# The chunked recurrence of a hybrid encoder block: one group for all transposes of a chunk, and a new order of the groups in a turn

## The chip, the cores and the metric

The kernel runs on one core of a Trainium2 chip. The metric is the device time of one execution in microseconds (us), here the median of three runs. The profile is one further execution with the hardware profiler on.

## The reference, cut to what matters

One layer for 2048 tokens of width 1024: a combined projection, then attention on one half of the columns and a recurrence (RWKV7) on the other, an output projection, and a mixture of experts. The change lies in the recurrence alone. For each of 8 heads (64 values, 64 keys) the reference steps through the tokens:

```
def step(state, inp):
    r_t, w_t, k_t, v_t, kk_t, b_t = inp
    sa = jnp.einsum('bhvk,bhk->bhv', state, -kk_t)
    state = (state * w_t[:, :, None, :] + sa[..., None] * b_t[:, :, None, :]
             + v_t[..., None] * k_t[:, :, None, :])
    return state, jnp.einsum('bhvk,bhk->bhv', state, r_t)
```

## The kernel before

The stages run one after the other: projection, attention, recurrence (`recur`), merge with the router, experts. Everything is float32.

`recur` cuts the 2048 tokens into 32 chunks of 64 (C = 64). Inside a chunk the recurrence is written as 64x64 matrix products: products of the chunk's own data, a triangular system that is solved by blocks and squarings (groups r1 to r8), and a few products with the running state. The eight heads are held as four pairs. Each product of one head works on 64 of TensorE's rows, and its result goes to 64 of its columns, so that several heads run at once in different quarters of the array. Products that contract over all 128 partitions use two column halves, and products with 128 result rows use two row halves. So there are three tile shapes: 64x64 (up to four at once), 64x128 (two at once) and 128x64 (two at once).

The work is laid out as a software pipeline. In turn k (k from -3 to 31) four chunks are in work: S_ = k (state step), B_ = k+1 and A_ = k+2 (two parts of the solve), N_ = k+3 (first products). A turn is full when all four exist, which holds for k = 0 to 28. The order of the groups in a turn is written by hand in `PE_TURN`, `ACT_TURN` and `DVE_TURN`. The code follows these orders, and each group of matmuls raises one semaphore at its last matmul. `counts` turns the orders into the semaphore values that the others wait for.

The groups, as the code of `turn` on TensorE has them:

| name | chunk | products | tile shape | reads, and who takes the result |
|---|---|---|---|---|
| s0 | B_ (before) | 8 | 64x64 | masked key term times values, opens the accumulation |
| s1 | S_ | 8 | 64x64 | adds state times A; ScalarE copies to sa0 |
| s2 | S_ | 8 | 64x64 | solve (q5) times sa0; ScalarE and VectorE copy to sv |
| s3 | S_ | 8 | 128x64 | tbk times sv; VectorE adds the old state (ds), then st scales it |
| y1, y2 | S_ | 8, 8 | 64x64, 128x64 | output term of the state, then of sv; ScalarE copies y |
| gl, gbk | N_ | 8, 8 | 64x64, 64x128 | first products; VectorE masks both (gl, g) |
| bk | A_ | 8 | 64x128 | transposes of B and K of a head together; ScalarE copies to tbk |
| v | A_ | 4 | 128x64 | transposes of V; ScalarE copies to sv |
| r1, r2, r3q, r3l, r4 | A_ | 16, 16, 8, 8, 8 | 64x64 | first part of the solve; copies and adds on ScalarE and VectorE |
| r5, r6, r7, r8 | B_ | 16, 8, 16, 8 | 64x64 | second part; r5 and r7 copied by ScalarE to ty, r6 and r8 added by VectorE |

Four PSUM tensors (ba, bb, bc, bd) of two banks each rotate by one place at each turn: what was bd is ba in the next turn, ba becomes bb, and bb becomes bc. r8 and r3l both write the low part of ba. gl of the next turn writes the same tensor under the name bb, and s0 of the next turn writes what r4 wrote as bd. This gives the waits:

```
if live(k):
    pe.wait_ge(s_dve, on_dve["r8", k])      # ahead of gl
...
if live(A_):
    pe.wait_ge(s_dve, on_dve["r4", A_])     # ahead of s0
```

GpSimd adds the identity to a part of g (`w0`) once a turn. SyncE loads a chunk's inputs into one of 5 buffers (`cin`) as soon as y1 and st of the chunk five earlier are done. Every product goes through the helper `product`, so all matmuls of the recurrence stand under line 937 in the profile; copies of ScalarE stand under L1112, additions of VectorE under L1147.

Of the kernel before, what the change touches and what calls it, by code (L numbers as in the profile page):

```python
# [24 lines left out]
P = 128  # L25
# [600 lines left out]
def attend(nc, io, dr, keep):  # L626
    with ExitStack() as ctx:
# [143 lines left out]
        def _(dve):  # L771
# [51 lines left out]
PE_TURN = (("s1", 0), ("gl", 3), ("r5", 1), ("gbk", 3), ("bk", 2), ("r1", 2), ("s2", 0), ("r2", 2), ("s3", 0), ("v", 2), ("r6", 1),  # L823
           ("r3q", 2), ("r3l", 2), ("r7", 1), ("y1", 0), ("r4", 2), ("y2", 0), ("r8", 1), ("s0", 1))
ACT_TURN = (("s1", 0), ("r5", 1), ("bk", 2), ("r1", 2), ("sa", 0), ("r2", 2), ("v", 2), ("r3l", 2), ("r7", 1), ("y", 0))
DVE_TURN = (("gl", 3), ("gbk", 3), ("sa", 0), ("r2", 2), ("s3", 0), ("r6", 1), ("st", 0), ("r3q", 2), ("r4", 2), ("r8", 1))
# [11 lines left out]
def recur(nc, io, dr, keep, ahead):  # L838
    with ExitStack() as ctx:
# [9 lines left out]
        tbk = [m.sb(f"tbk{n}", [P, 2, NPAIR, C]) for n in range(RINGS["tbk"])]  # L849
# [39 lines left out]
        def keys(couple):  # L889

            return couple.rearrange("p (r a) n -> p r (a n)", r=2)[:, :, 0:NPAIR * C]

        def values(couple, rows):

            return couple[rows, 1::2, 0:2 * C]

# [35 lines left out]
        def _(pe):  # L932
            A, R, V = slice(0, C), slice(C, 2 * C), slice(4 * C, 5 * C)
# [23 lines left out]

            def turn(k):
# [3 lines left out]
                ga, gn, gs = (g[c % RINGS["g"]] for c in (A_, N_, S_))  # L962
                if live(S_):
                    if S_ > 0:
                        pe.wait_ge(s_dve, on_dve["st", S_ - 1])
                    pe.wait_ge(s_pe, on_pe["s0", S_])
                    for p, r, f, t, u, j in by_features():
                        ins = product(ba[t, j, LO], xs[f, p, A], state[S_ % 2][f, p, :], False, not first(p))
                    ins.then_inc(s_pe, 1)
                if live(N_):  # L970
                    pe.wait_ge(s_ld[N_ % LOADS], 16 * (N_ // LOADS) + 16)
                    if live(k):
                        pe.wait_ge(s_dve, on_dve["r8", k])
                    for p, r, f, t, u, j in by_features():
                        ins = product(bb[t, j, LO], xn[f, p, A], xn[f, p, b_of(p)])
                    ins.then_inc(s_pe, 1)
                if live(B_):
                    pe.wait_ge(s_dve, on_dve["r4", B_])
                    if live(k - 1):
                        pe.wait_ge(s_act, on_act["y", k - 1])  # L980
                    elif live(k + 1):
                        pe.wait_ge(s_act, on_act["v", k + 1])
                    l = gl[B_ % RINGS["gl"]]
                    for p, r, f, t, u, j in by_features():
                        product(bc[f, p, LO], q2[t, j, :], eye[t, :])
                        ins = product(bc[f, p, HI], l[t, j, 1, :], q2[t, j, :])
                    ins.then_inc(s_pe, 1)
                if live(N_):
                    for p, r, f, t, u, j in by_features():
                        ins = product(whole(bd)[:, r, p, :], xn[f, p, BK], xn[f, p, AR])  # L990
                    ins.then_inc(s_pe, 1)
                if live(A_):
# [4 lines left out]
                    for p, r, f, t, u, j in by_features():  # L997
                        ins = product(keys(bb)[:, r, p * C:(p + 1) * C], xa[f, p, BK], eye[f, :])
# [20 lines left out]
                if live(A_):  # L1019
                    pe.wait_ge(s_act, on_act["r1", A_])  # L1020
                    pe.wait_ge(s_w0, A_ + 1)
                    if live(N_):
                        pe.wait_ge(s_dve, on_dve["gbk", N_])
                    w = w2[A_ % 2]
                    for q in range(2):
                        for r in range(2):
                            for h in range(2):
                                p, r, f, t, u, j = head(q + 2 * h, r)
                                product(bd[t, j, 0:2 * C], w[t, j, 0:C], w[t, j, C:3 * C])
                            for h in range(2):  # L1030
                                p, r, f, t, u, j = head(q + 2 * h, r)
                                ins = product(bd[t, j, 2 * C:3 * C], w[t, j, C:2 * C], w[t, j, 0:C])
                    ins.then_inc(s_pe, 1)
                if live(S_):
                    pe.wait_ge(s_act, on_act["sa", S_])
                    pe.wait_ge(s_dve, on_dve["sa", S_])
                    for p, r, f, t, u, j in by_features():
                        ins = product(ba[f, p, LO], tbk[S_ % RINGS["tbk"]][:, r, p, :], sv[S_ % RINGS["sv"]][:, p, features(r)])
                    ins.then_inc(s_pe, 1)
                if live(A_):  # L1040
                    for p in (0, 2, 1, 3):
                        u = HALVES[1 - p // 2]
                        ins = product(values(bb, u)[:, p % 2, :], xa[:, p, V], ident[:, :])
                    ins.then_inc(s_pe, 1)
                if live(B_):
                    pe.wait_ge(s_act, on_act["r5", B_])
                    if live(A_):
                        pe.wait_ge(s_act, on_act["r1", A_])
                    for p, r, f, t, u, j in by_features():
                        ins = product(bc[t, j, LO], ty[0][f, p, LO], ty[0][f, p, HI])  # L1050
# [12 lines left out]
                if live(B_):  # L1063
                    pe.wait_ge(s_dve, on_dve["r6", B_])
                    l = gl[B_ % RINGS["gl"]]
                    for p, r, f, t, u, j in by_features():
                        product(bc[f, p, LO], q3[t, j, :], eye[t, :])
                        ins = product(bc[f, p, HI], l[t, j, 2, :], q3[t, j, :])
                    ins.then_inc(s_pe, 1)
                if live(S_):  # L1070
                    if live(A_):
                        pe.wait_ge(s_act, on_act["v", A_])
                    for p, r, f, t, u, j in by_features():
                        ins = product(bb[f, p, LO], state[S_ % 2][f, p, :], xs[f, p, R], first(p), False)
                    ins.then_inc(s_pe, 1)
                if live(A_):
# [4 lines left out]
                    ins.then_inc(s_pe, 1)  # L1081
                if live(S_):
                    pe.wait_ge(s_pe, on_pe["y1", S_])
                    for p, r, f, t, u, j in by_features():
                        ins = product(bb[f, p, LO], sv[S_ % RINGS["sv"]][:, p, features(r)], gs[:, r, p, HI], False, not first(p))
                    ins.then_inc(s_pe, 1)
                if live(B_):
                    pe.wait_ge(s_act, on_act["r7", B_])
                    if not live(A_) and live(S_):
                        pe.wait_ge(s_dve, on_dve["s3", S_])  # L1090
                    for p, r, f, t, u, j in by_features():
                        ins = product(ba[t, j, LO], ty[1][f, p, LO], ty[1][f, p, HI])
                    ins.then_inc(s_pe, 1)
                    pe.wait_ge(s_act, on_act["v", B_])
                    if live(A_):
                        pe.wait_ge(s_dve, on_dve["r4", A_])
                    for p, r, f, t, u, j in by_tokens():
                        ins = product(bd[t, j, LO], g[B_ % RINGS["g"]][u, r, p, LO], sv[B_ % RINGS["sv"]][u, p, features(r)],
                                      first(p), False)
# [8 lines left out]
        def _(act):  # L1108
# [6 lines left out]
            def turn(k):  # L1115
                S_, B_, A_ = k, k + 1, k + 2
                ba, bb, bc, bd = banks(k)
                top, low = HALVES
                if live(S_):
                    copy("s1", S_, (sa0[:, :, :], ba[:, :, LO]))  # L1120
                if live(B_):
                    copy("r5", B_, (ty[0][:, :, :], bc[:, :, PAIR]))
                if live(A_):
                    copy("bk", A_, (tbk[A_ % RINGS["tbk"]].rearrange("p r a n -> p r (a n)"), keys(bb)))
# [4 lines left out]
                if live(A_):  # L1129
                    act.wait_ge(s_dve, on_dve["r2", A_])  # L1130
                    copy("r2", A_, (w4[:, :, :, :], bd.rearrange("p a (x y n) -> p a x y n", x=2, y=2)[:, :, :, 0, :]))
                    v = sv[A_ % RINGS["sv"]]
                    copy("v", A_, (v[low, 0:2, :], values(bb, low)), (v[top, 2:4, :], values(bb, top)))
                    copy("r3l", A_, (l8[:, :, :], ba[:, :, LO]))
                if live(B_):
                    copy("r7", B_, (ty[1][:, :, :], bc[:, :, PAIR]))
                if live(S_):
# [6 lines left out]
        def _(dve):  # L1144
# [4 lines left out]
            def turn(k):  # L1149
# [20 lines left out]
                if live(S_):  # L1170
                    add("s3", S_, ds_, ba[:, :, LO], state[S_ % 2])
                if live(B_):
                    add("r6", B_, q3, bc[:, :, LO], q2)
                if live(S_):
                    dve.wait_ge(s_dve, on_dve["s3", S_])
# [3 lines left out]
                if live(A_):  # L1179
                    dve.wait_ge(s_dve, on_dve["r2", A_])  # L1180
                    add("r3q", A_, q1, bd[:, :, LO], q0)
                    dve.wait_ge(s_dve, on_dve["r3q", A_])
                    add("r4", A_, q2, bd[:, :, LO], q1)
                if live(B_):
                    dve.wait_ge(s_dve, on_dve["r6", B_])
                    add("r8", B_, q5[B_ % 2], ba[:, :, LO], q3)

# [988 lines left out]
```

## Time and profile before

| | |
|---|---|
| median of three runs | 2983.03 us (2982.71 to 2984.04) |
| the profiled execution's own time | 2979.28 us |
| its span in the profile | 2977.3 us |
| mean granted TensorE clock | 0.981 of full speed |
| recurrence in the span | from about 1277 to 1680 us |
| state updates (st), first and last start | 1312.7 and 1679.5 us |
| a full turn | 12.04 us where nothing disturbs it |

The profiled execution agrees with the median within 0.13%. In the profile a matmul of float32 shows as two records, so a group of 8 products is x16. The line of a group names output, then moving operand, then stationary operand. PE is the matmul row of TensorE and PEld its weight loads. Ends of matmuls are modelled; starts are records.

### The profile page before, as it was taken

The page shows a single profiled execution, that of the slowest core. Times are in us where ns is not written, and L with a number is a line of the kernel's source. Part 1 is how long each engine was busy: PE and PEld are TensorE (multiplying, and loading weights), DVE is VectorE, ACT ScalarE, POOL GpSimd, SP SyncE. Part 2 cuts the span into 40 slices and gives each one's busy share as a digit, 9 for nine tenths or more (in the row PEclk, how much of TensorE's full clock was granted, in tenths as well). Part 3 has the DMA queues.
Part 4 walks back from the last instruction along what each step waited for, and adds up shares of the span by engine and source line. Part 5 has one row for each costly group of instructions (what it writes and reads, how often), then busy time and mean ns, then how long its engine had stood idle before and what let it go on. Part 6 is the DMA issues. An engine that isn't in the chain of part 4 may idle for free. (4 is left out here: it accounts for less than half of the span.)

```text
span 2977.3 us, 61430 instructions
## 1 busy us (share of the span) xinstructions
PE 2824.1 (95%) x23130; PEld 1777.5 (60%) x23131; DVE 1541.1 (52%) x3560; ACT 979.8 (33%) x2303; POOL 644.8 (22%) x812
## 2 busy tenths in 40 slices
PE   8999999999979999989999799994999999999999
PEld 6787878778756666679998555452333333333333
DVE  4677676777768988834444577763111111111111
ACT  3343344334437777734444333331000000000000
POOL 0000000000015555611111001002333333333333
PEclk9999999999989999999999999996999999999999
DMA  7111121121130110041111132253889788787663
GB/s 253 61 64 60 48 79 56 50 72 60 52 116 1 44 44 1 1 169 60 62 57 57 45 113 91 94 183 94 286 301 339 249 299 314 276 292 246 251 218 124
DMA packets 187586, 393.03 MB, mean 132 GB/s; under 512 B 15866, under 2 KB 74106, under 8 KB 186576
## 3 DMA queue, kind: packets, MB, share of 16 engines
q1 hardware_dynamic: 166848, 339.34, 33.0%
q0 software_dynamic: 20512, 50.54, 4.9%
q8 instruction: 159, 2.61, 0.4%
q14 instruction: 67, 0.55, 0.1%
HBM read 325.22 MB, written 78.22 MB: 136 GB/s over the span
## 5 line engine op out<-in xcount | busy, mean ns | idle before, releaser
L328 PE MATMUL pj_big<-pj_xnT,pj_w_in 128*128 128x256 f32 x2816 | 634.6, 381 | 2.1 <-DVE pj_xnT L467 1.5
L328 PEld LDWEIGHTS pj_big<-pj_xnT,pj_w_in 128*128 128x128 f32 x2816 | 537.0, 191 | 83.2 <-issue 5.7
L1921 PE MATMUL ex_pgu<-keep_res,ex_xT 128*64 128x512 f32 x2560 | 568.5, 597 | 0.0
L1921 PEld LDWEIGHTS ex_pgu<-keep_res,ex_xT 128*64 128x64 f32 x2560 | 177.1, 137 | 334.5 <-issue 334.5
L2029 DVE TENSOR_TENSOR ex_hh<-ex_sg,ex_pgu 128x256 f32<-128x256 f32 x80 | 33.7, 421 | 583.5 <-ACT ex_sg L1994 583.5
L1939 PE MATMUL ex_py<-keep_res,ex_hT 128*64 128x512 f32 x1280 | 288.3, 592 | 1.0 <-DVE ex_yb L2037 1.0
L767 POOL TENSOR_SCALAR at_tt<-at_e,at_cf 128x512 f32<-128x512 f32 (+3 forms) x160 | 219.7, 1376 | 176.7 <-DVE at_pd L811 164.1
L1440 PE MATMUL mg_po<-keep_res,mg_mix 128*128 128x512 f32 x512 | 232.5, 611 | 6.9 <-DVE mg_mix L1743 6.9
L298 POOL TENSOR_TENSOR pj_m<-pj_qn,pj_cosin 128x256 f32<-128x256 f32 x64 | 46.6, 729 | 823.4 <-DVE pj_qn L528 597.0
L1994 ACT ACTIVATE ex_sg<-ex_pgu 128x256 f32<-128x256 f32 x80 | 30.7, 384 | 581.4 <-PE ex_pgu L1921 581.4
L746 ACT ACTIVATE at_e<-at_sc,at_nmx 128x512 f32<-128x512 f32 (+3 forms) x320 | 197.0, 623 | 61.6 <-DVE at_nmx L789 59.3
L1939 PEld LDWEIGHTS ex_py<-keep_res,ex_hT 128*64 128x64 f32 x1280 | 91.9, 137 | 183.3 <-issue 182.1
L789 DVE TENSOR_REDUCE at_nmx<-at_sc 128x2 f32<-128x1024 f32 (+3 forms) x160 | 169.5, 1060 | 26.5 <-PE at_sc L708 17.8
L1440 PEld LDWEIGHTS mg_po<-keep_res,mg_mix 128*128 128x128 f32 x512 | 98.3, 196 | 124.1 <-issue 116.3
L1851 POOL DMA_INDIRECT ex_xb<-hn_s,ex_idx x80 | 82.5, 1031 | 361.4 <-PE ex_px L1914 351.0
L2037 DVE SCALAR_TENSOR_TENSOR ex_yb<-ex_py,ex_gates,ex_acc 128x512 f32<-128x512 f32 x80 | 60.1, 751 | 181.1 <-PE ex_py L1939 181.1
L732 PE MATMUL at_op<-at_vh,at_pt 128*128 128x128 f32 x1088 | 148.2, 276 | 0.8 <-ACT at_pt L758 0.8
L732 PEld LDWEIGHTS at_op<-at_vh,at_pt 128*128 128x128 f32 x1088 | 135.1, 193 | 1.4 <-ACT at_pt L758 1.0
L526 DVE RECIPROCAL pj_qrr<-pj_qrr 128x256 f32<-128x256 f32 x64 | 111.9, 1749 | 21.6 <-ACT pj_qrr L441 21.6
L1998 ACT ACTIVATE ex_hT<-ex_phT 128x256 f32<-128x256 f32 x80 | 30.7, 384 | 270.2 <-PE ex_phT L1929 270.2
L927 POOL TENSOR_TENSOR rw_w<-keep_first_head,rw_eye 64x256 f32<-64x256 f32 x64 | 46.1, 720 | 337.7 <-DVE keep_first_head L1158 335.8
L328 PE MATMUL pj_big<-pj_w_in,pj_xnT 128*128 128x512 f32 x256 | 112.5, 592 | 0.0
(288 smaller groups left out, 4370.7 us busy)
## 6 DMA issues: line engine op xcount, KB each, us to landing
keep_res<-in_w_exp_gate SPq DMA_DIRECT2D x32, 2048.0 KB, 8.9
keep_res<-in_w_exp_up SPq DMA_DIRECT2D x32, 2048.0 KB, 16.0
keep_res<-in_w_exp_down SPq DMA_DIRECT2D x32, 2048.0 KB, 8.7
chunks_s<-pj_st SPq DMA_DIRECT2D x32, 642.0 KB, 3.9
rw_cin<-chunks_s SPq DMA_DIRECT2D x32, 642.0 KB, 4.1
pj_xt<-in_x SPq DMA_DIRECT2D x20, 512.0 KB, 3.8
mg_xin<-in_x SPq DMA_DIRECT2D x8, 1024.0 KB, 7.3
out<-mg_hb SPq DMA_DIRECT2D x16, 512.0 KB, 3.4
```

Of the source, the lines that this page charges most:

```text
L298: pool.tensor_tensor(m1[:, p % 2, :], qn[:, p % 2, :], cosin[:, 0, :], ALU.mult).then_inc(s_m1, 1)
L328: ins = pe.matmul(out, lhs, rhs, start=(k == 0), stop=(k == KC - 1))
L526: link(dve, ch, dve.reciprocal(qrr[:, p % 2, :], qrr[:, p % 2, :]))
L732: ins = pe.matmul(op[t % 2][:, 0:P], pt[:, u % 2, b * P:(b + 1) * P], vh[h % 2][:, n, :], start=(n == 0), stop=(n == i))
L746: ins = act.activation(e[:, u % RE, c, 0:w], sc[u % 2][:, c, 0:w], ACT.Exp, bias=nmx[:, t % RE, c, s:s + 1], accum_out=sums[:, t % RE, c, ...
L767: pool.tensor_scalar(tt[:, u % 2, 0:w], e[:, u % RE, 1, 0:w], cf[:, t % RE, 1, s:s + 1], None, ALU.mult).then_inc(s_t, 1)
L789: dve.tensor_reduce(nmx[:, t % RE, :, s], sc[u % 2][:, :, 0:w], AX, ALU.max, negate=True)\
L1440: ins = pe.matmul(po[:, n, :], mix[:, x, k, tok], w_out[:, k, 512 * n:512 * n + 512], start=(k == 0), stop=(k == KC - 1))
L1851: pool.indirect_dma_start(xb[:, :], None, hn2, bass.IndirectOffsetOnAxis(idx[:, 0:1], 0), bounds_check=LAST, oob_is_err=False).then_inc(s_ ...
L1921: ins = pe.matmul(pgu[j * BT:(j + 1) * BT, :, :], lhs, wgu[x][:, k, :, j * HE:(j + 1) * HE], start=(k == 0), stop=(k == KC - 1))
L1939: ins = pe.matmul(py[n * BT:(n + 1) * BT, :], hT[:, part, j * BT:(j + 1) * BT], wd[x][:, 2 * j + part, n * HD:(n + 1) * HD], start=(part = ...
L2037: dve.scalar_tensor_tensor(yb[x][:, :], py[:, :], gates[:, bass.ds(b, 1)], acc[x][:, :], ALU.mult, ALU.add).then_inc(s_yb, 1)
```

## The change

- bk and v become one group, bkv: twelve transposes (B, K and V of each pair) through the 128x128 identity, all in the shape 128x64 with 128 moving columns. It stands where bk stood, ahead of r1. tbk gets the layout of sv. ScalarE copies it after sa, in three copies (two for V, one for B and K).
- s0 moves from the end of the turn before to the turn of its own chunk, behind gl and gbk.
- gl and gbk come first in the turn. s1 comes behind r5.
- y1 moves ahead of s3, and r6 ahead of y1. y2 follows s3 directly.
- r7 comes ahead of r3q and r3l. r8 follows r3l and r4 comes last. ScalarE copies r7 before r3l. VectorE adds r6 before s3, and r8 before r4.

```
-PE_TURN = (("s1", 0), ("gl", 3), ("r5", 1), ("gbk", 3), ("bk", 2), ("r1", 2), ("s2", 0), ("r2", 2), ("s3", 0), ("v", 2), ("r6", 1),
-           ("r3q", 2), ("r3l", 2), ("r7", 1), ("y1", 0), ("r4", 2), ("y2", 0), ("r8", 1), ("s0", 1))
-ACT_TURN = (("s1", 0), ("r5", 1), ("bk", 2), ("r1", 2), ("sa", 0), ("r2", 2), ("v", 2), ("r3l", 2), ("r7", 1), ("y", 0))
-DVE_TURN = (("gl", 3), ("gbk", 3), ("sa", 0), ("r2", 2), ("s3", 0), ("r6", 1), ("st", 0), ("r3q", 2), ("r4", 2), ("r8", 1))
+PE_TURN = (("gl", 3), ("gbk", 3), ("s0", 0), ("r5", 1), ("s1", 0), ("bkv", 2), ("r1", 2), ("s2", 0), ("r2", 2), ("r6", 1), ("y1", 0),
+           ("s3", 0), ("y2", 0), ("r7", 1), ("r3q", 2), ("r3l", 2), ("r8", 1), ("r4", 2))
+ACT_TURN = (("r5", 1), ("s1", 0), ("r1", 2), ("sa", 0), ("bkv", 2), ("r2", 2), ("r7", 1), ("r3l", 2), ("y", 0))
+DVE_TURN = (("gl", 3), ("gbk", 3), ("sa", 0), ("r2", 2), ("r6", 1), ("s3", 0), ("st", 0), ("r3q", 2), ("r8", 1), ("r4", 2))
...
-                    for p, r, f, t, u, j in by_features():
-                        ins = product(keys(bb)[:, r, p * C:(p + 1) * C], xa[f, p, BK], eye[f, :])
+                    for q in range(2):
+                        for column, swap, to in ((b_of, 0, PAIR), (k_of, 1, PAIR), (v_of, 1, PAIR2)):
+                            for h in range(2):
+                                p = q + 2 * h
+                                ins = product(bb[HALVES[h ^ swap], p, to], xa[:, p, column(p)], ident[:, :])
...
-                if live(A_):
-                    for p in (0, 2, 1, 3):
-                        u = HALVES[1 - p // 2]
-                        ins = product(values(bb, u)[:, p % 2, :], xa[:, p, V], ident[:, :])
...
+                if live(S_):
+                    if live(A_):
+                        pe.wait_ge(s_act, on_act["bkv", A_])
+                    for p, r, f, t, u, j in by_features():
+                        ins = product(bb[f, p, LO], state[S_ % 2][f, p, :], xs[f, p, R], first(p), False)
...
                 if live(B_):
+                    pe.wait_ge(s_act, on_act["r7", B_])
+                    if live(A_):
+                        pe.wait_ge(s_act, on_act["r3l", A_])
+                    elif live(S_):
+                        pe.wait_ge(s_dve, on_dve["s3", S_])
                     for p, r, f, t, u, j in by_features():
+                        ins = product(ba[t, j, LO], ty[1][f, p, LO], ty[1][f, p, HI])
```

## Rows read from the trace of the kernel before

**Rows 1.** The page, part 1 and part 6, the recurrence's loads.
```profile
PE 2824.1 (95%) x23130; PEld 1777.5 (60%) x23131; DVE 1541.1 (52%) x3560; ACT 979.8 (33%) x2303; POOL 644.8 (22%) x812
...
rw_cin<-chunks_s SPq DMA_DIRECT2D x32, 642.0 KB, 4.1
```

**Rows 2.** Stretches (windows): busy time of each engine, granted clock, DMA.
```profile
1400.00:1500.00 100.00, 96.72 (x2988) 90.18 (x2987) 44.55 (x91) 42.09 (x91) 11.52 (x16) 1.00 0.20 63
```

**Rows 3.** The state's tile: VectorE's updates, one a chunk.
```profile
L1176 DVE TENSOR_TENSOR rw_state<-rw_ds,rw_cin x32: 413/415/424, 1312.7 to 1679.5; 128x256 f32<-128x256 f32 x32
```

**Rows 4.** The timeline of one full turn, TensorE: start, us, what.
```profile
1450.87 0.46 PE L937 MATMUL rw_ps<-rw_state,rw_cin 64*64 64x64 f32 x16 [0.16 <-DVE rw_q L1147]
...
1451.13 0.44 PE L937 MATMUL rw_ps<-rw_cin 64*64 64x64 f32 x16
...
1451.36 0.33 PE L937 MATMUL rw_ps<-rw_eye,rw_q 64*64 64x64 f32 x6
...
1451.48 0.22 PE L937 MATMUL rw_ps<-rw_q,rw_gl 64*64 64x64 f32 x1
...
1452.07 1.16 PE L937 MATMUL rw_ps<-rw_cin 64*128 64x128 f32 x16
...
1453.06 1.01 PE L937 MATMUL rw_ps<-rw_eye,rw_cin 64*128 64x64 f32 x16
...
1454.00 0.33 PE L937 MATMUL rw_ps<-keep_first_head,rw_gl 64*64 64x64 f32 x4
...
1454.98 0.63 PE L937 MATMUL rw_ps<-rw_sa,rw_q 64*64 64x64 f32 x16
...
1455.85 1.55 PE L937 MATMUL rw_ps<-rw_w 64*64 64x128 f32 x32 [0.23 <-ACT rw_w L1112]
...
1457.33 0.69 PE L937 MATMUL rw_ps<-rw_sv,rw_tbk 128*64 128x64 f32 x16
...
1457.85 0.61 PE L937 MATMUL rw_ps<-rw_ident,rw_cin 128*64 128x128 f32 x8
...
1458.38 0.46 PE L937 MATMUL rw_ps<-rw_ty 64*64 64x64 f32 x16
...
1458.67 0.66 PE L937 MATMUL rw_ps<-rw_q,rw_w 64*64 64x64 f32 x16
...
1459.60 0.33 PE L937 MATMUL rw_ps<-rw_eye,rw_q 64*64 64x64 f32 x6
...
1461.21 0.69 PE L937 MATMUL rw_ps<-keep_first_head,rw_sv 128*64 128x64 f32 x16
...
1461.83 0.46 PE L937 MATMUL rw_ps<-rw_ty 64*64 64x64 f32 x16
...
1462.12 0.63 PE L937 MATMUL rw_ps<-rw_sv,keep_first_head 64*64 64x64 f32 x16
...
1462.91 0.46 PE L937 MATMUL rw_ps<-rw_state,rw_cin 64*64 64x64 f32 x16 [0.16 <-DVE rw_q L1147]
```

**Rows 5.** The same timeline, the copies and additions that TensorE may wait for.
```profile
1455.19 0.60 ACT L1112 ACTIVATE rw_w<-rw_ps 128x512 f32<-128x512 f32 x1 [0.48 <-PE rw_ps L937]
...
1457.45 0.42 DVE L1169 TENSOR_TENSOR rw_q<-rw_ps,rw_w 128x256 f32<-128x256 f32 x1 [1.36 <-PE rw_ps L937]
...
1458.53 0.77 ACT L1112 ACTIVATE rw_sv<-rw_ps 64x256 f32<-64x256 f32 x2
...
1459.83 0.38 ACT L1112 ACTIVATE rw_l<-rw_ps 128x256 f32<-128x256 f32 x1 [0.54 <-PE rw_ps L937]
...
1461.39 0.42 DVE L1147 TENSOR_TENSOR rw_q<-rw_ps,rw_q 128x256 f32<-128x256 f32 x1 [1.39 <-PE rw_ps L937]
...
1462.42 0.42 DVE L1147 TENSOR_TENSOR rw_q<-rw_ps,rw_q 128x256 f32<-128x256 f32 x1 [0.61 <-PE rw_ps L937]
```

**Rows 6.** Who waited for whom from 1316 to 1646 us: us in total, times, longest.
```profile
PEld rw_ps L937 <- ACT rw_w L1112: 9.8, 27, 0.4
...
PEld rw_ps L937 <- issue: 5.9, 31, 0.4
```

More of the change, by code:

```diff
@@ L848, in recur @@
         g = [old[:, n] for n in range(RINGS["g"])]
-        tbk = [m.sb(f"tbk{n}", [P, 2, NPAIR, C]) for n in range(RINGS["tbk"])]
+        tbk = [m.sb(f"tbk{n}", [P, NPAIR, 2 * C]) for n in range(RINGS["tbk"])]
         sv = [m.sb(f"sv{n}", [P, NPAIR, 2 * C]) for n in range(RINGS["sv"])]
@@ L887, in whole @@
             return couple.rearrange("p a n -> p (a n)").rearrange("p (r q n) -> p r q n", r=2, q=NPAIR)
[L889 to L895, printed above, removed]
         def split(ap):
@@ L932, in _ @@
         def _(pe):
-            A, R, V = slice(0, C), slice(C, 2 * C), slice(4 * C, 5 * C)
+            A, R = slice(0, C), slice(C, 2 * C)
             AR, BK = slice(0, 2 * C), slice(2 * C, 4 * C)
@@ L956, in b_of, with k_of, v_of @@
                 return slice(2 * C, 3 * C) if p < 2 else slice(3 * C, 4 * C)
+            def k_of(p):
+                return slice(3 * C, 4 * C) if p < 2 else slice(2 * C, 3 * C)
+            def v_of(p):
+                return slice(4 * C, 5 * C)
             def turn(k):
@@ L962, in turn @@
                 ga, gn, gs = (g[c % RINGS["g"]] for c in (A_, N_, S_))
+                if live(N_):
+                    pe.wait_ge(s_ld[N_ % LOADS], 16 * (N_ // LOADS) + 16)
+                    if live(k):
+                        pe.wait_ge(s_dve, on_dve["r8", k])
+                    for p, r, f, t, u, j in by_features():
+                        ins = product(bb[t, j, LO], xn[f, p, A], xn[f, p, b_of(p)])
+                    ins.then_inc(s_pe, 1)
+                    for p, r, f, t, u, j in by_features():
+                        ins = product(whole(bd)[:, r, p, :], xn[f, p, BK], xn[f, p, AR])
+                    ins.then_inc(s_pe, 1)
+                if live(B_):
+                    pe.wait_ge(s_dve, on_dve["r4", B_])
+                if live(S_):
+                    for p, r, f, t, u, j in by_tokens():
+                        ins = product(ba[t, j, LO], gs[u, r, p, LO], sv[S_ % RINGS["sv"]][u, p, features(r)], first(p), False)
+                    ins.then_inc(s_pe, 1)
+                if live(B_):
+                    if live(k - 1):
+                        pe.wait_ge(s_act, on_act["y", k - 1])
+                    else:
+                        pe.wait_ge(s_act, on_act["bkv", B_])
+                    l = gl[B_ % RINGS["gl"]]
+                    for p, r, f, t, u, j in by_features():
+                        product(bc[f, p, LO], q2[t, j, :], eye[t, :])
+                        ins = product(bc[f, p, HI], l[t, j, 1, :], q2[t, j, :])
+                    ins.then_inc(s_pe, 1)
                 if live(S_):
@@ L969, in turn @@
                     ins.then_inc(s_pe, 1)
[L970 to L973, printed above, removed]
-                    for p, r, f, t, u, j in by_features():
[L975 to L991, printed above, removed]
                 if live(A_):
@@ L996, in turn @@
                         pe.wait_ge(s_dve, on_dve["r8", S_])
-                    for p, r, f, t, u, j in by_features():
-                        ins = product(keys(bb)[:, r, p * C:(p + 1) * C], xa[f, p, BK], eye[f, :])
+                    for q in range(2):
[3 more added lines that the diff above has]
+                                ins = product(bb[HALVES[h ^ swap], p, to], xa[:, p, column(p)], ident[:, :])
                     ins.then_inc(s_pe, 1)
@@ L1033, in turn @@
                     ins.then_inc(s_pe, 1)
-                if live(S_):
+                if live(B_):
+                    pe.wait_ge(s_act, on_act["r5", B_])
+                    for p, r, f, t, u, j in by_features():
+                        ins = product(bc[t, j, LO], ty[0][f, p, LO], ty[0][f, p, HI])
+                    ins.then_inc(s_pe, 1)
+                if live(S_):
+                    if live(A_):
+                        pe.wait_ge(s_act, on_act["bkv", A_])
+                    for p, r, f, t, u, j in by_features():
+                        ins = product(bb[f, p, LO], state[S_ % 2][f, p, :], xs[f, p, R], first(p), False)
+                    ins.then_inc(s_pe, 1)
                     pe.wait_ge(s_act, on_act["sa", S_])
@@ L1037, in turn @@
                     for p, r, f, t, u, j in by_features():
-                        ins = product(ba[f, p, LO], tbk[S_ % RINGS["tbk"]][:, r, p, :], sv[S_ % RINGS["sv"]][:, p, features(r)])
+                        ins = product(ba[f, p, LO], tbk[S_ % RINGS["tbk"]][:, p, features(r)], sv[S_ % RINGS["sv"]][:, p, features(r)])
                     ins.then_inc(s_pe, 1)
-                if live(A_):
-                    for p in (0, 2, 1, 3):
-                        u = HALVES[1 - p // 2]
-                        ins = product(values(bb, u)[:, p % 2, :], xa[:, p, V], ident[:, :])
+                    pe.wait_ge(s_pe, on_pe["y1", S_])
+                    for p, r, f, t, u, j in by_features():
+                        ins = product(bb[f, p, LO], sv[S_ % RINGS["sv"]][:, p, features(r)], gs[:, r, p, HI], False, not first(p))
                     ins.then_inc(s_pe, 1)
                 if live(B_):
-                    pe.wait_ge(s_act, on_act["r5", B_])
-                    if live(A_):
-                        pe.wait_ge(s_act, on_act["r1", A_])
+                    pe.wait_ge(s_dve, on_dve["r6", B_])
+                    l = gl[B_ % RINGS["gl"]]
                     for p, r, f, t, u, j in by_features():
-                        ins = product(bc[t, j, LO], ty[0][f, p, LO], ty[0][f, p, HI])
+                        product(bc[f, p, LO], q3[t, j, :], eye[t, :])
+                        ins = product(bc[f, p, HI], l[t, j, 2, :], q3[t, j, :])
                     ins.then_inc(s_pe, 1)
@@ L1063, in turn @@
                 if live(B_):
-                    pe.wait_ge(s_dve, on_dve["r6", B_])
-                    l = gl[B_ % RINGS["gl"]]
-                    for p, r, f, t, u, j in by_features():
[L1067 to L1074, printed above, removed]
+                    pe.wait_ge(s_act, on_act["r7", B_])
[3 more added lines that the diff above has]
+                        pe.wait_ge(s_dve, on_dve["s3", S_])
+                    for p, r, f, t, u, j in by_features():
+                        ins = product(ba[t, j, LO], ty[1][f, p, LO], ty[1][f, p, HI])
                     ins.then_inc(s_pe, 1)
@@ L1080, in turn @@
                         ins = product(bd[t, j, LO], l8[t, j, :], q1[t, j, :])
[L1081 to L1099, printed above, removed]
                     ins.then_inc(s_pe, 1)
@@ L1118, in turn @@
                 top, low = HALVES
+                if live(B_):
+                    copy("r5", B_, (ty[0][:, :, :], bc[:, :, PAIR]))
                 if live(S_):
                     copy("s1", S_, (sa0[:, :, :], ba[:, :, LO]))
-                if live(B_):
-                    copy("r5", B_, (ty[0][:, :, :], bc[:, :, PAIR]))
                 if live(A_):
-                    copy("bk", A_, (tbk[A_ % RINGS["tbk"]].rearrange("p r a n -> p r (a n)"), keys(bb)))
                     copy("r1", A_, (w2[A_ % 2][:, :, PAIR], bc[:, :, PAIR]))
@@ L1129, in turn @@
                 if live(A_):
+                    v = sv[A_ % RINGS["sv"]]
+                    copy("bkv", A_, (v[low, 0:2, :], bb[low, 0:2, PAIR2]), (v[top, 2:4, :], bb[top, 2:4, PAIR2]),
+                         (tbk[A_ % RINGS["tbk"]][:, :, :], bb[:, :, PAIR]))
                     act.wait_ge(s_dve, on_dve["r2", A_])
                     copy("r2", A_, (w4[:, :, :, :], bd.rearrange("p a (x y n) -> p a x y n", x=2, y=2)[:, :, :, 0, :]))
-                    v = sv[A_ % RINGS["sv"]]
-                    copy("v", A_, (v[low, 0:2, :], values(bb, low)), (v[top, 2:4, :], values(bb, top)))
-                    copy("r3l", A_, (l8[:, :, :], ba[:, :, LO]))
                 if live(B_):
                     copy("r7", B_, (ty[1][:, :, :], bc[:, :, PAIR]))
+                if live(A_):
+                    copy("r3l", A_, (l8[:, :, :], ba[:, :, LO]))
                 if live(S_):
@@ L1169, in turn @@
                     dve.tensor_tensor(q0[:, :, :], bd[:, :, HI], w2[A_ % 2][:, :, W0], ALU.add).then_inc(s_dve, 1)
-                if live(S_):
-                    add("s3", S_, ds_, ba[:, :, LO], state[S_ % 2])
                 if live(B_):
@@ L1174, in turn @@
                 if live(S_):
+                    add("s3", S_, ds_, ba[:, :, LO], state[S_ % 2])
                     dve.wait_ge(s_dve, on_dve["s3", S_])
@@ L1181, in turn @@
                     add("r3q", A_, q1, bd[:, :, LO], q0)
-                    dve.wait_ge(s_dve, on_dve["r3q", A_])
-                    add("r4", A_, q2, bd[:, :, LO], q1)
                 if live(B_):
@@ L1186, in turn @@
                     add("r8", B_, q5[B_ % 2], ba[:, :, LO], q3)
+                if live(A_):
+                    dve.wait_ge(s_dve, on_dve["r3q", A_])
+                    add("r4", A_, q2, bd[:, :, LO], q1)
             dve.memset(state[0][:, :, :], 0.0).then_inc(s_init, 1)
```

## The prediction

> **What bounds the kernel now.** I read the page first: TensorE is busy for 95% of the span [rows 1]. The stretches then show the recurrence at 97% busy with the full clock (1.00, which is 2.4 GHz), while VectorE has 45%, ScalarE 42% and GpSimd 12% [rows 2]. The 32 state updates start from 1312.7 to 1679.5 us [rows 3]. That is 366.8 us for 31 turns, 11.8 on average with the shorter last ones. So the question is what TensorE spends in a turn of 12.04 us (1450.87 to 1462.91) [rows 4]. Nothing else in the kernel changes, and the merge starts when the recurrence has ended, so a difference in a turn is carried to the end of the kernel.
>
> The timeline of one turn gives the price of each group as the distance to the start of the next [rows 4]. Two prices recur. A group of 8 products in quarter or half tiles with 64 columns runs in rounds: r3q and r3l together take 0.93 (1458.67 to 1459.60), which is 0.47 each, 16 records in two tiles, so 8 rounds of 0.058. gl uses four tiles and takes 0.23, 4 rounds. With 128 columns, moving or stationary, a round costs about 0.11: gbk takes 1.00 for 8, v takes 0.54 for 4 with its exit. The second price is that of a change of tile shape. y2 should take 0.47 and takes 0.62 (1461.21 to 1461.83), and s3, which only enters, takes 0.52. So entering costs 0.05 in a slow first round and the gap ahead of the next shape is 0.10: 0.15 for one change.
>
> The rest is waiting. r1 ends its issue at 1454.98; ScalarE starts its copy 0.21 later, works 0.60, and r2 starts 0.06 after that, while s2 hides 0.47 [rows 4, 5]. This leaves 0.40 idle. s0 starts at 1462.12, is issued by 1462.59, and s1 starts at 1462.91: 0.32 idle, because s1 waits until s0 has finished (the row names VectorE, whose r8 addition ended just before). These two are the waits of a full turn.
>
> **The change, part by part, for a full turn.**
>
> *Transposes.* Removed are bk, 8 rounds (1453.06 to 1454.00, 0.94, of which 0.10 is the gap to the next shape: 0.84), and v, 4 rounds (0.54 less 0.10: 0.44), together 1.28. Added is bkv, twelve products of exactly v's form, 128x64 with 128 moving columns: 12 rounds of 0.109, 1.31. So the merge by itself costs +0.03. It needs no other data, and twelve transposes replace twelve.
>
> *Changes of shape.* Before, a turn has three blocks in another shape than 64x64: gbk with bk, s3 with v, and y2. After, it has three too: gbk, bkv, and s3 with y2. Six changes stay six: 0. The Trainium skill, page TensorEngine Tiling, section Key Properties, says that a change of tiling mode drains TensorE; the 0.15 per change agrees, and by that rule as well the sum is 0, since the count is equal.
>
> *s0 moved.* It now has r5 between itself and s1, 16 products, so s1 no longer waits: -0.32. s0's own wait for the r4 addition is hidden behind gl and gbk: the addition takes 0.42 and starts 0.3 after r4's issue, under 0.9 in all, against about 1.5 for gl and gbk. s0 is 8 products before and after.
>
> *r8 behind r3l.* r8 writes the same PSUM place as r3l and must wait until ScalarE has copied r3l. Before, r7 and y1 stood between. After, nothing does. r3l's issue ends at 1459.60, the copy starts at 1459.83, takes 0.38, and TensorE starts 0.05 later: 0.23 + 0.38 + 0.05 = 0.66 idle [rows 4, 5]. Queued behind r8 are r4 and the whole next turn. r7's own copy (0.60) is done by then, since r3q and r3l cover it with 0.93. New wait: +0.66.
>
> *gl behind r8 and r4.* gl writes the place from which VectorE adds r8. From r8's start to the addition's start is 0.59 (1461.83 to 1462.42), 0.42 for it, 0.05 to TensorE: 1.06 [rows 4, 5]. r8 and r4 cover 0.26 (s1's price after an idle time) + 0.47 = 0.73. New wait: +0.33. Before, s0 and s1 lay between, and the addition ended at 1462.84, no later than s1's own start.
>
> *Hidden parts.* bkv's three copies on ScalarE (0.77 for the two of V, 0.60) follow sa, so they end some 1.6 after r2's start; y1, which waits for them, would start after r2 (1.39) and r6 (0.23), at 1.62. This is cover of almost exactly the right length: I take 0.02; if it were gone, y1 would wait up to 0.2. The r2 copy, which starts only after VectorE's addition (1457.45 + 0.42), ends in time, because r6, y1, s3, y2 and r7 now stand between r2 and r3q. r6, s3 and st on VectorE keep their prices, with over 1 us of cover each. SyncE's load waits for y1 and st of the chunk five earlier; y1 comes earlier, st a little later, and a load takes 4.1 us of the two turns (24 us) that it has [rows 1]: 0. GpSimd waits for gbk's masking and works 1.5 us of a turn; r2 needs it one turn later: 0. The wait for r1's copy (0.40) stays, as r1, s2, r2 keep their order.
>
> *Small rest.* The order inside r5 and r7 (two products of one tile in a row) costs up to 0.12 and can fall elsewhere; I take +0.03.
>
> The sum for a full turn: +0.03 - 0.32 + 0.66 + 0.33 + 0.02 + 0.03 = +0.75 us. There are 29 full turns: +21.8. Turns -1 and 29 have the r8 wait too: +1.3. In the last three turns s0 stands right behind r4 and waits up to 0.8, and r8 of turn 30 waits for its copy, while y1 now fills waits for sa of 0.5 to 0.6; I estimate 0 net, between -2 and +2. The total is +23. The profiled execution's own 2979.3 becomes 3002.3; it lies 3.7 below the median, so the median goes from 2983.0 to 3006.
>
> **Unknown costs.** (a) bkv writes the lower, lower, upper halves in a row in places; no group before has this order with two column tiles. It costs nothing if TensorE takes a later product of the free tile first; in r5 it does: six matmuls with eye start ahead of the first with gl, though the code alternates them product by product [rows 4]. If the tile repeats stood in line, three of them would add 3 x 0.11 = 0.33 a turn. I take 0, by the r5 row; both ends stay, 0 to +9.6. The page TensorE: Matmul & The Clock Gate of the Trainium skill, section The mechanism, says that matmuls start in strict program order; the r5 row does not agree, and by the rule the time would be that of the second rival. (b) Waits for instructions ("issue") cost 5.9 us in 27 turns on the weight-load row [rows 6]; idle time elsewhere may absorb them: 0 to -4. I take 0.
>
> **The rivals.**
> - *The new waits are there, as forecast* (3006; own range 2998 to 3013).
> - *Second: bkv's repeats stand in line.* +0.33 in 29 turns on top: 3016. For it: nothing in v or bk shows such an order. Against: r5.
> - *Third: the waits are mostly covered.* If ScalarE's copy or VectorE's addition ran while TensorE still had queued work, one wait would vanish at a time; with the r8 wait gone the turn is +0.09 and the time 2983 + 3 = 2986, no change. Against: r1's copy, in the same position, leaves 0.40 idle in each of 27 turns [rows 6].
> - *Fourth, the other sign: TensorE is paced by the delivery of its instructions*, and the new waits only use time in which it would lag anyway, while the removed wait behind s0 was real. Then -0.32 + 0.03 in 29 turns, -8.4: 2975. It decides once over 0.7 of the 1.0 new idle time is absorbed. Against: the rounds keep 0.058 in every group, and issue waits are 0.2 a turn.
>
> **How the numbers follow.** Forecast 0.78, second rival 0.09, third 0.06, fourth 0.05, something else (slower) 0.02. The predicted time is the forecast's, 3006. The range from 2997 to 3015 holds the forecast's 0.78 nearly whole and about half of the second rival. A change of 0.2% (6 us) is what a measurement of this kernel can tell. Slower by more than that: 0.78 + 0.09 + 0.02 = 0.89 (a share of the third could join it); same 0.06; faster 0.05.
>
> **What the profile of the changed kernel would show.** Turns of 12.8 us; matmuls of the r8 group (rw_ty, x16) idle ahead of them about 0.6 with ScalarE's rw_l copy as the releaser; gl idle ahead 0.3 with VectorE as the releaser; s1 without the 0.32; bkv as 24 records that take 1.4 to the next group. The forecast is wrong if bkv's rounds are shorter than 0.11, if a change of shape costs less in the new places, or if a wait that I have as covered (y1 on bkv's copies first) is not.

## The result and the profile after

The changed kernel takes 3007.2 us (median of four runs, 3003.6 to 3011.9), the kernel before 2983.2. The ratio is 1.0082, with a 95% interval from 1.0070 to 1.0094: 24 us slower, and 3006 was forecast. The profiled execution took 3007.7 us at a span of 3005.8.

The recurrence accounts for it. It begins 1.9 us later than before, which no edit explains (the stages ahead of it are the same). From the first gl to the last state update it took 402.4 us (from 1277.1 to 1679.5, the first of these in the table of the run before). Now it takes 428.3, and behind it 0.7 is added. These are the page's row of TensorE, the row of gl and gbk of the cin tile, and the updates, which answer to [rows 1, 3]:

```profile
PE 2832.4 (94%) x23130; PEld 1779.3 (59%) x23131; DVE 1543.5 (51%) x3560; ACT 971.3 (32%) x2303; POOL 643.9 (21%) x812
```

```profile
L929 PE MATMUL rw_ps<-rw_cin x1024: 212/271/577, 1279.0 to 1672.8; 64*128 64x128 f32 x86, 64*64 64x64 f32 x85
...
L1169 DVE TENSOR_TENSOR rw_state<-rw_ds,rw_cin x32: 424/425/429, 1317.7 to 1707.3; 128x256 f32<-128x256 f32 x32
```

The number of matmuls is the same; from first to last update there are 389.6 us instead of 366.8. The stretch that answers to [rows 2] shows TensorE less busy at the same full clock:

```profile
1400.00:1500.00 100.00, 92.08 (x2792) 84.89 (x2792) 42.07 (x84) 37.43 (x85) 11.55 (x16) 1.00 0.16 50
```

The timeline of an undisturbed turn, from r2 to the next r2 (TensorE unless another engine is named; start, us, what; it answers to [rows 4, 5]):

```profile
1470.24 1.49 PE L929 MATMUL rw_ps<-rw_w 64*64 64x128 f32 x29 [0.23 <-ACT rw_w L1105]
...
1471.15 0.58 ACT L1105 ACTIVATE rw_tbk<-rw_ps 128x512 f32<-128x512 f32 x1
...
1471.86 0.63 PE L929 MATMUL rw_ps<-rw_cin,rw_state 64*64 64x64 f32 x16
...
1472.43 0.69 PE L929 MATMUL rw_ps<-rw_sv,rw_tbk 128*64 128x64 f32 x16
...
1472.94 0.64 PE L929 MATMUL rw_ps<-keep_first_head,rw_sv 128*64 128x64 f32 x16
...
1473.51 0.36 PE L929 MATMUL rw_ps<-rw_eye,rw_q 64*64 64x64 f32 x8
...
1475.23 0.39 ACT L1105 ACTIVATE rw_l<-rw_ps 128x256 f32<-128x256 f32 x1 [0.29 <-PE rw_ps L929]
...
1475.76 0.46 PE L929 MATMUL rw_ps<-rw_ty 64*64 64x64 f32 x16 [0.57 <-ACT rw_l L1105]
1476.02 0.68 PE L929 MATMUL rw_ps<-rw_q,rw_l 64*64 64x64 f32 x16
1476.35 0.87 DVE L1141 TENSOR_TENSOR rw_q<-rw_ps,rw_q 128x256 f32<-128x256 f32 x2 [1.09 <-PE rw_ps L929]
1476.92 1.55 PE L929 MATMUL rw_ps<-rw_cin 64*64 64x64 f32 x32 [0.23 <-DVE rw_q L1141]
...
1478.41 0.51 PE L929 MATMUL rw_ps<-rw_sv,keep_first_head 64*64 64x64 f32 x10
...
1479.83 1.53 PE L929 MATMUL rw_ps<-rw_ident,rw_cin 128*64 128x128 f32 x24
...
1481.29 0.33 PE L929 MATMUL rw_ps<-keep_first_head,rw_gl 64*64 64x64 f32 x4
...
1482.27 0.63 PE L929 MATMUL rw_ps<-rw_sa,rw_q 64*64 64x64 f32 x16
...
1483.13 1.11 PE L929 MATMUL rw_ps<-rw_w 64*64 64x128 f32 x20 [0.23 <-ACT rw_w L1105]
```

The turn is 12.89 us (1470.24 to 1483.13). r8 (rw_ty, 1475.76) stands idle 0.57 for ScalarE's copy of r3l. gl (1476.92) comes 0.43 after r4 could have been issued (1476.02 + 0.47). s1 no longer has a gap. The twelve transposes are 24 records and take 1.46 to r1, in place of 0.94 and 0.53. (The idle shown in a row starts at the modelled end of the last matmul, so it is less than the loss counted from issue to issue.)

### The profile page after: what moved, and what is told of

Read it like the earlier page. It is cut to its first block and busy times, and to the rows that moved or that the text cites. A ratio compares the mean times of both kernels' runs of the same rounds, so it can differ in the third digit from the quotient of the medians.

```text
span 3005.8 us, 61368 instructions
## 1 busy us (share of the span) xinstructions
PE 2832.4 (94%) x23130; PEld 1779.3 (59%) x23131; DVE 1543.5 (51%) x3560; ACT 971.3 (32%) x2303; POOL 643.9 (21%) x812
```

## The experiments

The theory: a turn is the sum of the groups' prices and of each wait whose chain is longer than the work put in between; r8 behind r3l and gl behind r8 cost what the removed wait of s1 doesn't give back. The rivals: repeats of a column half cost time in bkv; the instruction delivery paces TensorE, so that idle time is free; one tile shape for all transposes is a gain that the new order hides.

"Turn" is the recurring distance between the same instruction of two turns; "31 turns" is the first to the last state update. The ratio is to the kernel before on the same chip, with its 95% interval.

| kernel | turn, us | 31 turns, us | median, us | ratio |
|---|---|---|---|---|
| before | 12.03 | 366.8 | 2983.2 | 1 |
| changed | 12.89 | 389.6 | 3007.2 | 1.0082 (1.0070 to 1.0094) |
| gl_free | 12.43 | 375.8 | 2989.6 | 1.0032 (1.0020 to 1.0045) |
| r8_gl_free | 12.18 | 370.1 | 2979.0 | 0.9995 (0.9986 to 1.0005) |
| alternate | 12.89 | 389.2 | 3003.0 | 1.0074 (1.0057 to 1.0091) |
| wait_order | 12.72 | 383.3 | 2999.9 | 1.0059 (1.0045 to 1.0073) |
| merge_alone | 12.65 | 382.9 | 2995.6 | 1.0050 (1.0033 to 1.0067) |
| s1_only | 12.12 | 369.0 | 2985.0 | 1.0007 (0.9998 to 1.0016) |
| s1_r8 | 11.65 | 359.3 | 2972.7 | 0.9967 (0.9955 to 0.9979) |
| filled | 11.58 | 357.2 | 2972.7 | 0.9968 (0.9956 to 0.9980) |

The kernel before ran beside them at 2980.0 us (gl_free, r8_gl_free, alternate, merge_alone) and 2981.9 us (wait_order, s1_only, s1_r8, filled); so the ratios are to be compared, not the medians.

**gl_free and r8_gl_free: take the new waits away.**

```
-    ins = product(ba[t, j, LO], ty[1][f, p, LO], ty[1][f, p, HI])      # r8
+    ins = product(bc[t, j, LO], ty[1][f, p, LO], ty[1][f, p, HI])
...
-    if live(k): pe.wait_ge(s_dve, on_dve["r8", k])                     # ahead of gl
+    if live(k): pe.wait_ge(s_dve, on_dve["r8", k])                     # ahead of gbk
...
-    pe.wait_ge(s_act, on_act["r3l", A_])                               # ahead of r8, r8_gl_free only
```

> The changed kernel with r8 writing to bc, which is free once ScalarE has copied r7, instead of ba; r8 still waits for the copy of r3l. gl has no wait for r8's addition any more, gbk has it instead. Theory (gl's wait is a real loss of 0.43 us a turn as the trace has it): a full turn falls from 12.89 to about 12.5 us, the kernel by 29 x 0.4 = 12 us, to about 2995. Rival (TensorE is paced by the delivery of its instructions, idle time is absorbed): the turn stays near 12.9 and the kernel within 3 us of the changed one.

> As gl_free, and r8 no longer waits for the copy of r3l; only r4 does, which needs it. Theory (each wait costs what its chain is longer than the work in between): r8's 0.23 us now lies inside the wait for r3l's copy, so r4 idles about 0.5 us where r8 idled 0.7, and gl does not idle: a full turn of about 12.2 to 12.3 us, the kernel near 2988. If the new waits are the whole loss, what is left over the kernel before (12.03 us a turn) is r4's wait less the removed wait of s1. Rival (instruction delivery): no change from 12.9.

The first gives 12.43, so the wait of gl was 0.46 us of each turn. The timeline of gl_free shows gl following r4 with no idle time (two of its records, from 1476.88, start before r4's last three), while r8 still waits:

```profile
1476.27 0.46 PE L929 MATMUL rw_ps<-rw_ty 64*64 64x64 f32 x16 [0.57 <-ACT rw_l L1105]
1476.53 0.57 PE L929 MATMUL rw_ps<-rw_q,rw_l 64*64 64x64 f32 x13
...
1476.88 0.27 PE L929 MATMUL rw_ps<-rw_cin 64*64 64x64 f32 x2
```

The second gives 12.18. r8 now starts before the copy, and the rest of the wait moves to r4, which needs the copied data:

```profile
1474.43 0.46 PE L929 MATMUL rw_ps<-rw_ty 64*64 64x64 f32 x16
1474.68 0.38 ACT L1101 ACTIVATE rw_l<-rw_ps 128x256 f32<-128x256 f32 x1 [0.30 <-PE rw_ps L929]
...
1475.20 0.59 PE L929 MATMUL rw_ps<-rw_q,rw_l 64*64 64x64 f32 x13 [0.31 <-ACT rw_l L1101]
```

Together they give back 0.71 of the 0.86 us, and the kernel can't be told from the one before. The loss is in the two waits. If idle time were absorbed by the delivery of instructions, neither would have moved the turn.

**alternate: the order of the twelve transposes.**

```
-    for h in range(2):
+    for h in (0 ^ swap, 1 ^ swap):
```

> The changed kernel with the twelve transposes written so that the two column halves alternate strictly; nothing else differs. Theory (TensorE takes a later product of the free tile first, the repeats cost nothing): turn 12.89 us as before, kernel within 1 us of the changed one's. Rival (repeats of a tile stand in line, 3 x 0.11 us a turn): turn 12.56 us, kernel faster by 9.6 us.

The turn is 12.89, the same, and the 24 records again take 1.46:

```profile
1462.08 1.53 PE L929 MATMUL rw_ps<-rw_ident,rw_cin 128*64 128x128 f32 x24
1463.54 0.33 PE L929 MATMUL rw_ps<-keep_first_head,rw_gl 64*64 64x64 f32 x4
```

The repeats cost nothing.

**merge_alone: only the transposes, in the kernel before.** bk becomes bkv in its place, v is gone, and ScalarE copies bkv after sa; the rest of the order is the old one.

```
-("bk", 2), ("r1", 2), ("s2", 0), ("r2", 2), ("s3", 0), ("v", 2), ("r6", 1),
+("bkv", 2), ("r1", 2), ("s2", 0), ("r2", 2), ("s3", 0), ("r6", 1),
```

> The kernel before with only the transposes merged (bkv in the place of bk, its copies after sa, v gone); s0, s1, y1, r8 stay where they were. Theory: the rounds stay 12, but gbk and bk no longer share a shape and s3 stands alone, so a turn has one change of shape more (+0.15) and the twelve rounds cost +0.03; the wait of r3q for the r2 copy is no longer covered by v's 0.44 (+0.3 to +0.5 us). In all a turn of 12.5 to 12.7 us, the kernel about 3000. Rival (one tile shape for all transposes saves time by itself): a turn of less than 12.0 us, the kernel faster than 2983.

12.65, 0.62 more. The timeline says where:

```profile
1401.32 0.69 PE L937 MATMUL rw_ps<-rw_sv,rw_tbk 128*64 128x64 f32 x16
...
1401.90 0.60 ACT L1118 ACTIVATE rw_w<-rw_ps 128x512 f32<-128x512 f32 x1 [0.58 <-DVE rw_q L1175]
1401.94 0.46 PE L937 MATMUL rw_ps<-rw_ty 64*64 64x64 f32 x16
...
1402.64 0.68 PE L937 MATMUL rw_ps<-rw_q,rw_w 64*64 64x64 f32 x16 [0.24 <-ACT rw_w L1118]
...
1408.10 1.16 PE L937 MATMUL rw_ps<-rw_cin 64*128 64x128 f32 x16
...
1409.19 1.53 PE L937 MATMUL rw_ps<-rw_ident,rw_cin 128*64 128x128 f32 x24
```

r6 takes 0.70 to r3q instead of 0.29, because r3q waits for the r2 copy that v had covered: +0.41. s3 takes 0.62 (0.52 before) and gbk 1.09 (0.99 before), since each now changes shape alone: +0.20. bkv itself (1.46) costs what bk and v cost (0.94 and 0.53). So one tile shape saves nothing, and taking v away from behind s3 costs. In the changed kernel r3q has no such wait, since y1, y2 and r7 stand in v's place.

**wait_order: where a late wait stands.** The two waits ahead of gl change places, and r8's first wait, which the second implies, is dropped. In the traces the wait written first is carried by the group's first weight load, and the second stands in an instruction of its own.

```
-    pe.wait_ge(s_ld[N_ % LOADS], 16 * (N_ // LOADS) + 16)
     if live(k): pe.wait_ge(s_dve, on_dve["r8", k])
+    pe.wait_ge(s_ld[N_ % LOADS], 16 * (N_ // LOADS) + 16)
...
-    pe.wait_ge(s_act, on_act["r7", B_])
     if live(A_):
         pe.wait_ge(s_act, on_act["r3l", A_])
-    elif live(S_):
-        pe.wait_ge(s_dve, on_dve["s3", S_])
+    else:
+        pe.wait_ge(s_act, on_act["r7", B_])
+        if live(S_):
+            pe.wait_ge(s_dve, on_dve["s3", S_])
```

> The changed kernel with the same two waits ahead of gl in the other order (r8's addition first, the load second), and without r8's wait for the copy of r7, which the later wait for the copy of r3l implies. Theory (the late wait stands in an instruction of its own ahead of the matmul and so costs 0.1 us more than one that the matmul carries; the trace has 0.15 from the addition's end to gl and 0.14 from the copy's end to r8, against 0.05 behind r1's copy): the turn falls by 0.1 to 0.2 us, the kernel by 3 to 6 us. Rival (the 0.15 is the latency of this pair of engines): no change.

The turn falls by 0.17, and r8 starts 0.05 after the copy's end (1473.95 + 0.38), not 0.14. From r8 to gl there are 1.08 us, not 1.16:

```profile
1473.95 0.38 ACT L1106 ACTIVATE rw_l<-rw_ps 128x256 f32<-128x256 f32 x1 [0.30 <-PE rw_ps L929]
1474.38 0.46 PE L929 MATMUL rw_ps<-rw_ty 64*64 64x64 f32 x16 [0.47 <-ACT rw_l L1106]
...
1475.46 1.55 PE L929 MATMUL rw_ps<-rw_cin 64*64 64x64 f32 x32
```

In the view of waits from 1316 to 1646 us, the weight loads' time put down to "issue" (waits for nothing that the profile shows) falls from 14.2 to 5.2 us (the first row is the changed kernel, the second wait_order):

```profile
PEld rw_ps L929 <- issue: 14.2, 53, 0.7
```

```profile
PEld rw_ps L929 <- issue: 5.2, 27, 0.8
```

So about 9 us of "issue" in the changed kernel were these waits.

**s1_only, s1_r8, filled: the same ideas in the kernel before.** s1_only puts s1 behind gl and r5. s1_r8 adds r8 in bc, as in gl_free. filled moves r6 between s2 and r2 as well (written to bb), r7 ahead of r3q, and r8 and r4 between y1 and y2.

```
 s1_only, s1_r8: PE_TURN = (("gl", 3), ("r5", 1), ("s1", 0), ("gbk", 3), ("bk", 2), ...
 filled: ... ("r1", 2), ("s2", 0), ("r6", 1), ("r2", 2), ("s3", 0), ("v", 2), ("r7", 1), ("r3q", 2), ("r3l", 2),
         ("y1", 0), ("r8", 1), ("r4", 2), ("y2", 0), ("s0", 1))
```

> The kernel before with s1 moved behind gl and r5, nothing else. Theory: s1's wait of 0.32 us for s0 is gone, but gl now comes straight after s0 and waits for r8's addition (r8's start + 1.1 us against 0.76 of cover, 0.3 to 0.4 us): a turn of 12.0 to 12.1 us, the kernel the same within 3 us. Rival (the wait behind s0 is no real loss): the turn grows to 12.4 and the kernel by 10 us.

> As s1_only, with r8 writing to bc, so that gl has no wait for its addition (gbk has it). Theory: both waits are gone, a turn of 11.7 us, the kernel near 2974. Rival (instruction delivery): 12.0 us a turn, no change.

> As s1_r8, and r6 moved between s2 and r2, where TensorE idles 0.40 us for r1's copy (it writes to bb, which is free there); r7 comes ahead of r3q, r8 and r4 between y1 and y2. Theory (a turn is the sum of the groups' prices and the waits whose chain is longer than the work put in between): r1's wait falls to about 0.17 us, r3q, r4 and s0 wait at most 0.1 each: a turn of 11.3 to 11.5 us, the kernel 2960 to 2966. Rival (instruction delivery or an unseen wait bounds the turn): not under 11.7.

s1_only: 12.12, a little above the expectation: one wait went, gl's came, and gl's carries the extra 0.1 of a separate wait. s1_r8: 11.65, as expected, and faster than both kernels (0.9967). The expectation for filled failed: 11.58, not 11.3 to 11.5, and the kernel is no faster than s1_r8. Its timeline shows the new order's own waits at the end of the turn:

```profile
1363.42 0.38 ACT L1115 ACTIVATE rw_l<-rw_ps 128x256 f32<-128x256 f32 x1 [0.30 <-PE rw_ps L937]
...
1363.95 0.68 PE L937 MATMUL rw_ps<-rw_q,rw_l 64*64 64x64 f32 x16
1364.56 0.69 PE L937 MATMUL rw_ps<-keep_first_head,rw_sv 128*64 128x64 f32 x16
1365.31 0.51 PE L937 MATMUL rw_ps<-rw_sv,keep_first_head 64*64 64x64 f32 x10
```

r4 starts 0.15 after the end of the r3l copy. y2 takes 0.75 to s0, against 0.62 to r8 before, since s0 waits for r4's addition. The 0.23 won behind s2 is mostly given back there. What remains of the difference was not tried.

## Why the prediction was right, point by point

- **A full turn: forecast +0.75, measured +0.86.** The mechanism is the one forecast, and two terms of the sum were too small (below). The prices of most groups held: r2 and r6 take 1.62 to y1 (forecast 1.62), gl and gbk 1.49 to s0 (about 1.5), bkv 1.46 with entry and exit (1.31 + 0.15).
- **Transposes +0.03 and changes of shape 0.** Right: alternate and merge_alone bear both out, the latter by adding a change of shape and paying for it.
- **s1's wait, -0.32.** Right: s1_r8, which has this and no wait in its place, gains 0.38.
- **r8 behind r3l, +0.66.** Mis-sized by 0.1. The copy starts at 1475.23, takes 0.39, and r8 starts 0.14 after its end; with the forecast's 0.23 from the end of r3l's issue to the copy (its last record starts at 1474.98) the wait is 0.76. The forecast had 0.05 in place of 0.14. It doesn't show in full in the turn, because r7, r3q and r3l take 1.49 with the entry (1473.51 to 1475.00), where the rows of before give 1.55 (r7, y1 and r4 together 1.61, less 0.10 for the exit and 0.94 for y1 and r4; 0.93 for r3q and r3l; 0.05 for the entry).
- **gl behind r8, +0.33.** Mis-sized: 0.43 in the trace, 0.46 by gl_free. The chain from r8 to gl is 1.16 us (1475.76 to 1476.92), not 1.06. The missing 0.1, here and in the r8 term, is the wait that stands in an instruction of its own, as wait_order shows: it takes 0.09 off the one and 0.08 off the other. The kernel before has such a wait too, ahead of s1 (1462.80 in its trace), where I had taken it as part of s0's completion.
- **The whole kernel: forecast +23, measured +24 of the medians.** A hit within 1 us is in part luck. The profiled executions differ by more, 28.5 in span: the recurrence grew by 25.9, and 1.9 and 0.7 stand before and behind it. Of the 25.9, 22.8 lie between the first and the last state update. The 28 distances between updates of full turns add 24.1 at 0.86 each; turns that something stretched cost 4.1 us before and 2.5 after; the last three distances add 0.4. The other 3.1 lie between the first gl and the first update. There the profiled execution of the changed kernel stopped once for 1.62 us and soon after ran at a granted clock of 0.50 (1.2 GHz) for a while:

```profile
1298.14 0.33 PE L929 MATMUL rw_ps<-keep_first_head,rw_gl 64*64 64x64 f32 x4 [1.62 <-issue]
```

```profile
1300.60:1303.80 3.20, 2.65 (x71) 2.46 (x69) 0.85 (x2) 0.81 (x3) 0.00 (x0) 0.50 1.10 350
```

alternate, which has the same order of groups, kept the full clock there and takes 35.9 us, the kernel before 35.6, the changed one 38.7. So the full turns alone are 3.2 us dearer than forecast (29 at 0.11), and the +1.3 for turns -1 and 29 can't be told apart from such stops; that the medians come to +24 doesn't confirm it.

- **The rivals.** The repeats in bkv cost nothing (alternate). The waits are not covered. The pace of instruction delivery did not absorb the new idle time; what there is to it stands below. The rule of the Trainium skill, page TensorE: Matmul & The Clock Gate, section The mechanism, that matmuls start in strict program order would have given 3016; the turn of 12.89 us with the repeats and without them doesn't agree with it.

r8_gl_free can't be told from the kernel before, though its turn is 0.15 longer. Over the 31 turns it lies 3.3 us above, but the spans of the profiled executions differ by only 1.6 (2978.9 and 2977.3), and the interval of the ratio ends at +1.5 us.

## What to carry to other kernels

When a software pipeline is reordered, list for each group what it waits for, and add up the chain of that wait against the groups now in between. Fewer and more uniform groups were worth nothing by themselves here: count the rounds and the changes of shape before and after. Where a group waits only for a place in PSUM and not for data, another place may be free: here it was worth 0.46 us a turn. When a group of matmuls has two waits, see to it that its first instruction carries the late one itself; here that is the one written first.

## What the runs showed of the hardware that I had not expected

A wait in an instruction of its own ahead of the matmul costs TensorE 0.1 us more than one that the group's first weight load carries: in the changed kernel r8 and gl start 0.14 and 0.15 us after the end of the awaited work, in wait_order 0.05 and 0.06.

TensorE stops at times with nothing to wait for, and most in the kernels with the shortest turns. In filled it stopped in the middle of a group of sixteen for 1.33 us:

```profile
1473.14 0.55 PE L937 MATMUL rw_ps<-rw_eye,rw_cin 64*128 64x64 f32 x7
...
1475.02 0.77 PE L937 MATMUL rw_ps<-rw_eye,rw_cin 64*128 64x64 f32 x9 [1.33 <-issue]
```

In s1_r8 such waits total 3.1 us on the matmul row (5 times, up to 1.2 us) from 1316 to 1646 us, and in the kernel before 0.5 us. This fits with s1_r8's gain: 28 full turns at 0.38 would be 10.6 us, and first to last update it is 7.5, since stretched turns cost it 7.6 us, and the kernel before 4.1. A short turn isn't needed, though: r8_gl_free, with 12.18 us a turn, has a stop of 1.35 us, and the kernel before has two of 1.1 us ahead of its first state update.

The traces point at instruction fetch. Packets of 16 KB on the instruction queue (q8) start every 4.0 us in filled (median); ahead of its stops of 1.33 and 0.85 us the next one came only after 6.6 and 6.3 us (1466.0 to 1472.6, 1551.4 to 1557.8), and TensorE went on 1.4 us after it had landed. In all ten profiles each of the 35 "issue" stops over 0.25 us on the matmul row, from 1290 to 1665 us, ends 1.2 to 1.6 us after the landing of such a packet. No run changed the fetch, so this is read from the order in time alone, and why some packets start late stays open. The Trainium skill, page Runtime: NRT & Kernel Launch, section Instruction fetch mechanics, says that instruction fetch is hidden behind dispatch in straight code; this case's trace doesn't agree in these places.

A stop can cost more than its length. After the stop in filled the granted clock was 0.50 (1.2 GHz) from 1476.5 to 1479.9, and the thirty-two records of r2 took 2.33 us in place of 1.55:

```profile
1477.00:1478.00 1.00, 1.00 (x33) 1.00 (x32) 0.00 (x0) 0.60 (x1) 0.00 (x0) 0.50 0.00 0
```

```profile
1478.17 2.33 PE L937 MATMUL rw_ps<-rw_w 64*64 64x128 f32 x32
```

From one state update to the next 14.61 us went by there, not 11.58. The stops of 1.35 us in r8_gl_free and 1.23 us in s1_r8 were not followed by a lower clock; what decides it stays open.
